# Routing in batches beside the projection, and experts' outputs added to the output in memory

## The reference, cut to what matters

```
h2 = (_rms(x, p['norm_ffn']) * (1.0 + sc2) + sh2).astype(dt)
x = x + (g2 * _moe(h2, p)).astype(dt)

# in _moe
g_sel = argmax(g_logits);  g_prob = softmax(g_logits)[g_sel]
top_v, top_i = lax.top_k(e_in, TOP_K)            # 2 experts of the group
gates = jax.nn.softmax(top_v, axis=-1) * g_prob
rank = ... cumsum(onehot) ...                    # place of a row in its expert's list
# blocks of MOE_BLK = 128 rows, one expert each
out = (jax.nn.silu(xb @ wg[e]) * (xb @ wu[e])) @ wd[e]
y = y.at[slot_tok].add(out * slot_w[:, None])
```

## Time and profile before

| | us |
|---|---|
| median of 3 runs (lowest, highest) | 2757.96 (2756.16, 2759.23) |
| profiled execution's own time | 2750.47 |
| its span | 2748.8 |
| PE busy | 2351.7 (86%) |
| DVE busy | 927.5 (34%) |
| ACT busy | 534.6 (19%) |
| POOL busy | 221.1 (8%) |

### The profile page before, as it was taken

One profiled execution on the slowest core, in us unless ns is written; L12 is line 12 of the kernel. 1 busy time (PEld: TensorE's weight loads), 2 busy tenths in 40 slices (PEclk: granted clock), 3 DMA queues, 4 the chain that ended last, 5 costly groups with the idle time before them and its releaser, 6 DMA issues. The chain is left out here.

```text
span 2748.8 us, 26852 instructions
## 1 busy us (share of the span) xinstructions
PE 2351.7 (86%) x7602; PEld 1157.2 (42%) x7603; DVE 927.5 (34%) x2008; ACT 534.6 (19%) x986; POOL 221.1 (8%) x328
## 2 busy tenths in 40 slices
PE   4798999998786989999999329999999999999910
PEld 1344555444443545455545114444444444444400
DVE  4655632046622334454445611111111111111138
ACT  3400101364322223343333000100000000001000
POOL 0001011000102000000000150000000000000023
PEclk8899999999997878998999659999999999999955
DMA  9142233359966232121243504575377886867458
GB/s 382 52 161 56 64 68 132 114 198 271 334 207 198 90 142 76 45 87 43 102 140 110 207 24 147 214 277 187 142 292 270 321 329 228 334 264 302 177 191 347
DMA packets 132155, 503.28 MB, mean 183 GB/s; under 512 B 16299, under 2 KB 54923, under 8 KB 111771
## 3 DMA queue, kind: packets, MB, share of 16 engines
q1 hardware_dynamic: 97728, 360.32, 35.8%
q0 software_dynamic: 23024, 100.46, 11.1%
q10 hardware_dynamic: 11312, 41.36, 3.7%
HBM read 379.69 MB, written 124.18 MB: 183 GB/s over the span
## 5 line engine op out<-in xcount | busy, mean ns | idle before, releaser
L2312 PE MATMUL bank<-arena 128*128 128x512 f32 x1120 | 490.5, 594 | 14.3 <-issue 14.3
L2012 PE MATMUL bank<-arena 128*128 128x512 f32 (+1 forms) x960 | 360.0, 535 | 19.5 <-ACTq L942 19.5
L2312 PEld LDWEIGHTS bank<-arena 128*128 128x128 f32 x1120 | 211.9, 190 | 288.9 <-issue 288.9
L2233 PE MATMUL bank<-arena 128*128 128x512 f32 (+1 forms) x544 | 265.0, 624 | 0.0
L2340 PE MATMUL bank<-arena 128*128 128x512 f32 x560 | 251.7, 602 | 10.1 <-issue 10.0
L2012 PEld LDWEIGHTS bank<-arena 128*128 128x128 f32 x960 | 168.8, 192 | 206.8 <-issue 185.7
L1898 DVE COPY arena<-bank 128x512 f32<-128x512 f32 x50 | 34.6, 693 | 576.9 <-PE bank L2327 576.9
L2340 PEld LDWEIGHTS bank<-arena 128*128 128x128 f32 x560 | 104.1, 191 | 134.9 <-issue 131.8
L2145 PE MATMUL bank<-arena 64*128 64x256 f32 (+3 forms) x256 | 143.7, 650 | 9.8 <-SPq L411 9.8
L1630 DVE CUSTOM_DVE_ANT_0 arena<-bank,arena 128x256 f32<-128x256 f32 (+3 forms) x128 | 58.3, 456 | 267.9 <-PE bank L2145 252.8
L2233 PEld LDWEIGHTS bank<-arena 128*128 128x128 f32 (+1 forms) x544 | 98.2, 195 | 93.1 <-issue 92.1
(11 more groups left out here) (446 smaller groups left out, 2596.3 us busy)
## 6 DMA issues: line engine op xcount, KB each, us to landing
arena<-wg SPq DMA_DIRECT2D x32, 2048.0 KB, 12.6
arena<-wu SPq DMA_DIRECT2D x32, 2048.0 KB, 16.2
arena<-wd SPq DMA_DIRECT2D x32, 2048.0 KB, 8.8
ye_d<-arena SPq DMA_DIRECT2D x11, 3072.0 KB, 20.6
ye_d<-arena ACTq DMA_DIRECT2D x50, 512.0 KB, 8.3
arena<-mod_w SPq DMA_DIRECT2D x12, 2048.0 KB, 13.1
z_d<-arena ACTq DMA_DIRECT2D x12, 1056.0 KB, 6.5
arena<-z_d POOLq DMA_DIRECT2D x10, 1056.0 KB, 12.9
```

The costliest lines, as they stand in the source:

```text
L2012: ins = mm(bank[n % 2][:, 0:w], wz[:, i % 3, k, :], hT[:, k, t0:t0 + w], start=(k == 0), stop=(k == KT - 1))
L2233: ins = mm(bank[5 + q][0:r], l, wo[:, k, 512 * q:512 * q + 512], start=(k == 0), stop=(k == KT - 1))
L2312: ins = mm(bank[bk][:, :], xgT[:, s, k, :], m[:, w, k, :], start=(k == 0), stop=(k == KT - 1))
```

## The change

- Each expert gets a fixed region of `tok_d` (RUNB = 17 blocks), so a row's place no longer depends on the other experts' counts. Routing then runs in five batches, of four tiles and a last one of one tile, as steps `r0`, `r1`, `r2`, `re`, `rk`, `r3`, `r4`, `sc`: group, first and second expert, exponentials, ranks, gates, slots, scatter. Batches 0 to 3 lie among the rows of the projection, batch 4 after the last logits, followed by `ut`, which makes the table of units (on 128 partitions, one per unit, turned by one transpose).
- A slot holds four words: row of `h2`, row of the output, gate, row of `g2`. It is preset for unused slots, which point to 128 extra rows of the output.
- `row_out` stores `x1` straight to the output `y`.
- In the loop GpSimd now gathers the rows, gathers each slot's `g2` row (`factors`), reads the table of a later unit (`load`) and adds the scaled rows to the output with an accumulating indirect DMA (`add`), one after another. VectorE scales by gate and `g2`. At the end of a pair GpSimd waits for its gathers and tables. For an unused pair it issues two small DMAs in a chain (`over`).
- The steps `bar 2`, `bar 3`, `comb`, the zero fills of `ye_d` and its stores are gone. The weights of expert 0 are loaded at tile row 9, those of expert 1 after the last logits.

```diff
+            if (i, j) == (7, 0):
+                out.append(("rinit",))
+            if (i, j) == (9, 5):
+                out.append(("pre",))
+            return out + ROUTE.get((i, j), [])
+        RSTEPS = ["r0", "r1", "r2", "re", "rk", "r3", "r4", "sc"]
+        for b, i in ((0, 8), (1, 10), (2, 13), (3, 17)):
+            for j, names in ((2, RSTEPS[:1]), (4, RSTEPS[1:2]), (6, RSTEPS[2:4])):
+                ROUTE.setdefault((i, j), []).extend((f, b) for f in names)
+            for j, names in ((0, RSTEPS[4:6]), (2, RSTEPS[6:])):
+                ROUTE.setdefault((i + (b < 3), j if b < 3 else 7), []).extend((f, b) for f in names)
+        ROUTE.setdefault((NT + 1, 2), []).extend([("w1",)] + [(f, 4) for f in RSTEPS] + [("ut",)])
-        SCHEDULE += [("bar", 2), ("route",), ("moe",), ("bar", 3), ("comb",)]
+        SCHEDULE += [("moe",)]
...
+                def load(n, s):
+                    r = entry(pool, blk, n, 0, NBLK - 1)
+                    pool.dma_start(tk[:, s].unsqueeze(1), tok_v[:, bass.ds(r, 1), :]).then_inc(S(f"ld_tk{s}"), 16)
...
+                def factors(n, s):
+                    pool.tensor_copy(cur[:, s], tk[:, s, 1:4]).then_inc(S("cur_copied"), 1)
...
+                    pool.indirect_dma_start(out=g2x[:, s], out_offset=None, in_=g2_d,
+                                            in_offset=bass.IndirectOffsetOnAxis(ap=cur[:, s, 2:3], axis=0)).then_inc(S(f"ld_g2{s}"), 16)
+                def add(n, s):
+                    pool.wait_ge(S("yV"), n + 1)
...
+                    pool.wait_ge(S("yH"), n + 1)
+                    if not (isinstance(n, int) and n == 0):
+                        pool.sem_inc(S("xg_turn"), 1)
+                        pool.wait_ge(S("acc"), n * 16)
...
+                    pool.tensor_copy(sidx[:, s:s + 1], cur[:, s, 0:1]).then_inc(S("sid_copied"), 1)
...
+                    pool.indirect_dma_start(out=O["y"], out_offset=bass.IndirectOffsetOnAxis(ap=sidx[:, s:s + 1], axis=0),
+                                            in_=yb[:, s], in_offset=None, compute_op=ALU.add).then_inc(S("acc"), 16)
                 def body(it):
-                    if isinstance(it, int) and it == LAST:
-                        return
+                    last = isinstance(it, int) and it == LAST
                     for s in range(2):
-                        pair(it * 2 + 2 + s, s, it + 1)
+                        n = it * 2 + s
+                        if not last:
+                            gather(n + 2, s, it + 1)
+                        add(n, s)
+                        if not last:
+                            factors(n + 2, s)
+                            load(n + 4, s)
+                    if not last:
+                        for s in range(2):
+                            pool.wait_ge(S(f"ld_xg{s}"), it * 16 + 32)
...
+                            pool.wait_ge(S(f"ld_g2{s}"), it * 16 + 32)
...
+                            pool.wait_ge(S(f"ld_tk{s}"), it * 16 + 48)
...
+                def over(it):
+                    for s in range(2):
+                        pool.wait_ge(S("acc"), it * 32 + 16 * s)
+                        pool.sem_inc(S("xg_turn"), 1)
+                        pool.dma_start(idle, sidx[0:1, :]).then_inc(S("acc"), 16)
...
+                        STT(yb[rr, s, 0:512], bank[4][rr, :], curf[rr, s, 1:2], g2x[rr, s, 0:512], ALU.mult, ALU.mult).then_inc(S("yH"), 1)
+                        dve.wait_ge(S("yA"), n + 1)
+                        STT(yb[rr, s, 512:1024], yb[rr, s, 512:1024], curf[rr, s, 1:2], g2x[rr, s, 512:1024], ALU.mult, ALU.mult).then_inc(S("yV"), 1)
```

More of the change, by code:

```diff
@@ L428, in skipped, with groups, other @@
                 eng.sem_inc(S(name), n)
-        def groups(eng, body, signals):
+        def groups(eng, body, signals, over=None):
+            def other(it):
+                skipped(eng, signals(it))
+                if over is not None:
+                    over(it)
             body(0)
@@ L437, in groups @@
                 with eng.Else():
-                    skipped(eng, signals(it))
+                    other(it)
             with eng.If(entry(eng, used, LAST * 2) > 0):
@@ L441, in groups @@
             with eng.Else():
-                skipped(eng, signals(LAST))
+                other(LAST)
         block = ctx.enter_context(nc.Block())
@@ L640, in route @@
                 sp.sem_inc(S("h2_stored"), 1)
+                sp.wait_ge(S("b7_free"), B7["l", NT - 1] + 1)
+                weights_of(1, None)
             def moe(step):
[L643 to L652, removed]
+                sp.wait_ge(S("route_done"), 1)
+                for e in range(2, NE):
+                    weights_of(e, entry(sp, wfree, e - 2, 1, NPAIR + 1))
                 for name in ("wg", "wu", "wd"):
@@ new lines, in moe @@
+                pool.wait_ge(S("route_done"), 1)
+                pool.wait_ge(S("st_tok"), 16 * 2 * NT)
+                load(0, 0)
+                load(1, 1)
+                pool.wait_ge(S("h2_stored"), 1)
+                for s in range(2):
+                    gather(s, s, None)
+                for s in range(2):
+                    factors(s, s)
+                    load(2 + s, s)
+                def over(it):
+                    for s in range(2):
+                        pool.wait_ge(S("acc"), it * 32 + 16 * s)
+                        pool.sem_inc(S("xg_turn"), 1)
+                        pool.dma_start(idle, sidx[0:1, :]).then_inc(S("acc"), 16)
@@ L1073, in bar @@
                         act.wait_ge(S(f"st_v{q}"), 16 * (9 - q))
-                if n == 3:
-                    for q in range(2):
-                        act.wait_ge(S(f"st_ye{q}"), 16 * NPAIR // 2)
                 barrier(act)(step, n)
@@ L1839, in route @@
-                dve.sem_inc(S("dest_ready"), 1)
-                link(dve.tensor_copy(dest, slot[:, 0]))
-                def over(ap):
-                    return ap[0:1].unsqueeze(1).broadcast_to([1, NPAIR, 32])
-                first = bc(blk0[0:1], 32)
-                ex_, fl, end, z4 = (zsum[0:1, n] for n in range(4))
-                dve.wait_ge(S("h2_stored"), 1)
-                link(TT(cmpc[0:1], over(ends), first, ALU.is_le))
-                link(dve.tensor_reduce(ex_, cmpc[0:1], AX.X, ALU.add))
```

500 lines of the change are left out of this document (265 added, 235 removed).

## The result

The changed kernel takes 3311.38 us (median of 4 runs, 3307.83 to 3320.26) against 2758.6 for the kernel before (4 runs, 2756.16 to 2762.83), a ratio of 1.2007 with an interval of 1.1977 to 1.2036. It is slower, as forecast, but by 553 us where 162 were forecast, and outside the range. Its profiled execution took 3320.26 us, with a span of 3318.7 and a mean granted clock of 0.849.

A forecast was written before the change was run, and what follows sets the result against it. It took TensorE to bound the experts' loop, with 218.5 us of routing and combining almost without matrix work. Sum: 2750.5 + 10 - 58 + 199 + 55 + 15 - 62 = 2909.5, plus 7.5, rounded to 2920 us; range 2780 to 3080.

The forecast's parts named there:

- Its size on an undisturbed queue, 199: Experts' loop: TensorE's waits for late row gathers sum to 199 us, before any competition from weight loads.
- the split by the pair's end and by half units: Loop: even gathers, after GpSimd's wait at the pair's end, land at 17.7 us, odd at 13.1; up hides 14.4 or 7.6.
- The earlier start of the loop: Routing: batches beside the projection add 10 us; the shorter serial part after it brings first transposes 58 us earlier.
- The end: After the loop: combining's 122.57 us goes; last unit's 10 and eight skipped pairs' 50 replace it; net -62 us.
- The weights' loads compete: Loop: weight loads run while addition and factors are under way; mostly covered by issue times, 15 us added (0 to 50).
- the other rule of that page: GpSimd's queue: descriptors start in order, so the gather's data stand behind the addition's; 199 us with it, 149 without.
- The clock term: Loop: TensorE's clock falls to 0.50 after long waits; 16 waits at 2.6 us, fifteen at perhaps 1, 55 us in all.
- The addition is slow: Rival, loop: addition takes 8 us or more of data, GpSimd's chain sets the period, 360 instead of 199; 3080 and above; 0.17.
- a sign against itself: Loop: a landing of the addition over 10 us would show the prediction wrong.
- The clock does not recover between waits: Rival, loop: part of TensorE's 961.59 us of work runs at clock 0.50; a fifth adds 190, giving 3110; chance 0.06.
- Faster, because the gather is hardly late: Rival, loop: every gather lands 12.6 us after the down product, so only 14 half units wait; 2740 us; chance 0.13.
- waits of 10 us and more in the projection: Projection, where routing batches are interleaved: such waits would show the prediction wrong.

The follow-up runs named there:

- e_early: Changed kernel with the rows of unit n+4 gathered ahead of addition n and tables read two units earlier, all work kept; 2652.79 us.
- a_noweights: Changed kernel with only 8 KB of each weight matrix loaded for experts 2 to 31, so their products use stale weights; 3046.74 us.
- f_skip: Changed kernel without the small chained DMAs of unused pairs; GpSimd waits for the additions at each used pair's end instead; 3288.76 us.
- i_split: Changed kernel with each 2 MB weight load issued as four DMAs of 4 KB per partition instead of one of 16 KB; 3217.03 us.
- c_nofactors: Changed kernel with factors gathered for the first two units only and those used throughout; 3173.62 us.
- k_before_late: Kernel before the change, each gather held until VectorE is done with the unit before, nothing in front of it in the queue; 2891.17 us, ratio 1.0498.
- b_plain: Changed kernel with the transfer to the output writing instead of adding, so the output is not the sum over experts; 3222.37 us.

## Why the prediction was wrong in size

**Right, by the experiments.** The mechanism: the gather comes after the down product, behind addition, factors and table, and TensorE waits for rows. e_early issues the gather a pair earlier and the waits are gone. Its size on an undisturbed queue, 199, was 228.7 in a_noweights, and it fits there class by class, not only in the sum (mean wait of a unit in us, forecast and measured; in the last row the sum of two):

| gather, up that hides it | units | forecast | a_noweights | changed kernel |
|---|---|---|---|---|
| even, full | 15 | 3.3 | 4.3 | 9.3 |
| even, half | 9 | 10.1 | 10.1 | 15.5 |
| odd, full | 19 | 0 | 0.3 | 5.0 |
| odd, half | 5 | 5.5 | 6.8 | 14.4 |
| last two together | | 30 | 32.7 | 33.3 |

So the split by the pair's end and by half units is right, and the weights add 5 to 8 us to a unit of every class. (By the forecast's own parts two of its landings are 0.2 us low: 10.4 and 0.9 give 11.3, 12.4 and 0.9 give 13.3. That would add about 6 us.)

**Right, by the traces.** The earlier start of the loop: -48 forecast (+10 and -58), -46.7 measured. The parts are near too: the last h2 operation ended 14.7 us later than before where 10 were forecast, and from it to the first row transposes it is 61.4 us less where 58 were forecast.

**Right in the sum, in part by luck.** The end: -62 forecast, -63.7 measured. The forecast had 10 us for the last addition and 50 for the skipped pairs, 6.2 each. Without the tiny transfers the end still takes 28.7 us (f_skip), so they account for about 30; they follow one another at about 2.15 us, three at 2.7 to 3.5, sixteen of them. Two errors of some 20 us cancel.

**The step that failed** is "The weights' loads compete: ... Most is covered by issue times; I add 15 (0 to 50)". It cost 250 us: 479 in 45 waits with the weights, 228.7 without them. The reason given was that issue times cover the competition. They don't: by the worst landings above a transfer lands 6 to 10 us later with the loads than without, and the row gather, the last of the four, is no exception. A late landing reaches TensorE in both kinds of unit, in one as the gather's own, in the next as that of factors and table, for which GpSimd waits before it issues the gather. The figure stood in the earlier trace rows, a worst landing of 12.1 us against the usual 4.4; the forecast used it as a bound for the addition only. i_split takes 104 of these 250 us back with loads in packets of 4 KB. The Trainium skill, in DMA: Bandwidth & Descriptors, section "Queues, rings and completion order", has this rule: each DMA engine goes round the queues that have work and takes a whole packet from one before it turns to the next. By that rule a packet of GpSimd's queue waits for a larger one of the weights, and i_split's fall of 104 us agrees. On the other rule of that page, which the prediction weighed, that one queue's descriptors start in order, c_nofactors bears: with the factors' gather gone from in front of it the table read lands at worst in 11.1 us instead of 15.1, which agrees. But the order alone does little here: behind the same three transfers the row gather lands within 5.8 us when no weights are loaded.

**The clock term was mis-sized.** "Some 16 waits over 5 us cost 16 x 2.6 = 42, fifteen of 3.3 us perhaps 1 each: 55 in all" measured 137. There were 45 waits, not 31, and the mean cost in busy time is 3.0 us a wait (137/45). In k_before_late waits of 2 us in the mean cost 2.2 (47/21), so short ones, with the late start behind them, do not cost "perhaps 1". The bound from the earlier trace rows, 2.6 us, was nearly right for each; the number of waits, and the 1 us for short ones, were not.

**A term was missing.** After a wait the down product starts late, 1.4 to 1.8 us in full units and 1.5 to 2.5 in half ones, with "issue" as what ended it: idle time other than for rows rose from 31.8 to 95.8 us (574.8 less 479), by 64. k_before_late has it too (48), e_early hardly (7.6: its idle time after the first transposes is 39.4). That TensorE's sequencer, held at the row transposes, has no lead left for the register loads ahead of the down product, is argued from where it appears; it was not tried by itself.

So the loop, by terms: waits 199 forecast, 229 measured; weights 15 and 250; clock 55 and 137; late starts 0 and 64. Sum 269 and 680. The last three terms hold 381 of the 411 that are missing. Low clock and late starts go with the number of waits more than with their length: in a_noweights, with half the waiting in 39 waits, they still cost 110 and 74 us.

**The rivals.** "The addition is slow" had the sign and the size that came nearest (3080 and above), but not as told: b_plain shows that adding costs 90 us of waits. It lands in 7.9 us median; 16 of 50 land above the 10 that the prediction named as a sign against itself, 13.2 at worst, but without the weights none takes more than 6.7. It is the loads that hold it up. "The clock does not recover between waits" was wrong as a mechanism: it recovers within each down product. "Faster, because the gather is hardly late" asked for a queue that does not hold the gather back and a pair's end that is covered. a_noweights has the first, landings of at most 5.8 us, and still 228.7 us of waits, 188 of them in even units and the last two: the pair's end is not covered. As the prediction's last part said, waits of 10 us and more in the projection would speak against it: there was one, of 14.29 us.

Not tried: the new routing alone with the old combining stage; and the change with its tables and factors on another queue, which the order of the gathers made needless.

## What to carry to other kernels

Before a transfer is added to a queue, ask what it is put in front of: the same additions, factors and tables that cost 553 us ahead of the row gather give 100 us less than the kernel before when the gather goes first. Price a queue's transfers as they run beside the large loads of the stage, not as they land alone: here 3.5 us became 9.3 in the median and 15.1 at worst. Ask what a gather fetches: the one of factors brought 512 KB a unit from nine rows and cost 126 us of waits. And count waits, not only their sum: for each one the loop lost 4.5 us more than the wait itself in low clock and late starts, in the mean and even where the waits were 2 us long.
